# Compressed scores of two heads in one product of 64 columns, and the first operand parts of causal attention made in front of one meeting instead of two

## What is computed

```python
s = jnp.einsum('bqghd,bngd->bghqn', qb, k_cmp) * scale
p_cmp = _masked_softmax(s - slopes * dist, dist >= 0)
o_cmp = jnp.einsum('bghqn,bngd->bqghd', p_cmp.astype(v_cmp.dtype), v_cmp)
...
s = jnp.einsum('bqghd,bgqmd->bghqm', qb, k_sel) * scale
p = _masked_softmax(s - slopes * dist, dist >= 0)
o_slc = jnp.einsum('bghqm,bgqmd->bqghd', p.astype(v_sel.dtype), v_sel)
...
s = jnp.einsum('bqghd,bkgd->bghqk', qb, kw) * scale
p = _masked_softmax(s - slopes * wd.astype(jnp.float32), wmask)
o_win = jnp.einsum('bghqk,bkgd->bqghd', p.astype(vw.dtype), vw)
o = gb[..., 0:1] * o_cmp + gb[..., 1:2] * o_slc + gb[..., 2:3] * o_win
```

## Time and profile before

| | us |
|---|---|
| median of 3 runs | 3345.44 |
| lowest and highest of them | 3343.83, 3346.9 |
| the profiled execution | 3342.76 |
| its span in the trace | 3341.0 |
| PE busy in the span | 3247.5 (97%) |
| DVE, ACT, POOL busy | 1785.4 (53%), 1297.1 (39%), 205.7 (6%) |

### The profile page before, as it was taken

One profiled execution on the slowest core, in us unless ns is written; L12 is line 12 of the kernel. 1 busy time (PEld: TensorE's weight loads), 2 busy tenths in 40 slices (PEclk: granted clock), 3 DMA queues, 4 the chain that ended last, 5 costly groups with the idle time before them and its releaser, 6 DMA issues.

```text
span 3341.0 us, 41312 instructions
## 1 busy us (share of the span) xinstructions
PE 3247.5 (97%) x15343; PEld 2620.3 (78%) x15343; DVE 1785.4 (53%) x2671; ACT 1297.1 (39%) x1849; POOL 205.7 (6%) x230
## 2 busy tenths in 40 slices
PE   8989998999999999999999999999999999999998
PEld 6668976888888888876688888888888668888887
DVE  7357696445553455335765555345553566555532
ACT  4227755233332333323266333333322325633332
POOL 1001100000000000010110000010000011010000
PEclk9959999999999999999999999999999999999999
DMA  5320033333333333332312333333333322233332
GB/s 127 87 67 1 2 82 87 94 94 94 98 96 93 95 94 99 93 106 70 76 30 69 99 91 97 92 98 93 97 93 96 84 58 53 64 95 94 94 93 65
DMA packets 518489, 276.53 MB, mean 83 GB/s; under 512 B 39499, under 2 KB 510383, under 8 KB 518226
## 3 DMA queue, kind: packets, MB, share of 16 engines
q1 hardware_dynamic: 513154, 262.77, 28.6%
q0 software_dynamic: 3840, 11.26, 1.4%
q10 hardware_dynamic: 1360, 0.66, 0.1%
HBM read 264.11 MB, written 2.14 MB: 80 GB/s over the span
## 4 chain that ended last, share of the span: by engine, by line
PE 89%; DVE 7%; ACT 2%; issue 1%; DVEq 0%; DMA 0%; POOL 0%; ACTq 0%; POOLq 0%
PE bank L375 25%; PE bank L377 24%; PE bank L376 24%; PE bank L968 5%; PE bank L949 4%; PE bank L957 3%; PE bank L2386 1%; DVE wlo L351 1%; PE bank L1685 1%; PE bank L2359 1%; PE bank L2371 0%; DVE xc L1891 0%; DVE std L2571 0%; PE bank L687 0%; PE bank L1704 0%
## 5 line engine op out<-in xcount | busy, mean ns | idle before, releaser
L375 PE MATMUL bank<-hhi,whi 128*128 128x512 f32 (+1 forms) x2504 | 991.9, 396 | 7.5 <-DVE wlo L351 5.1
L377 PE MATMUL bank<-hlo,whi 128*128 128x512 f32 (+1 forms) x2504 | 977.0, 390 | 0.0
L376 PE MATMUL bank<-hhi,wlo 128*128 128x512 f32 (+1 forms) x2504 | 976.7, 390 | 0.0
L351 DVE TENSOR_TENSOR wlo<-raw,whi 128x1024 fp32r<-128x1024 f32 x485 | 608.9, 1258 | 585.0 <-ACT whi L344 576.2
L344 ACT CAST whi<-raw 128x1024 fp32r<-128x1024 f32 x485 | 505.1, 1046 | 408.6 <-PE bank L377 395.0
L375 PEld LDWEIGHTS bank<-hhi,whi 128*128 128x128 f32 (+1 forms) x2504 | 470.6, 188 | 147.3 <-issue 43.5
L376 PEld LDWEIGHTS bank<-hhi,wlo 128*128 128x128 f32 (+1 forms) x2504 | 470.7, 188 | 99.6 <-issue 3.4
L377 PEld LDWEIGHTS bank<-hlo,whi 128*128 128x128 f32 (+1 forms) x2504 | 470.1, 188 | 100.3
L375 PE MATMUL bank<-uhi,whi 128*128 128x512 f32 x880 | 348.6, 396 | 0.0
L376 PE MATMUL bank<-uhi,wlo 128*128 128x512 f32 x880 | 348.0, 395 | 0.0
L377 PE MATMUL bank<-ulo,whi 128*128 128x512 f32 x880 | 348.0, 395 | 0.0
(11 more groups left out here) (444 smaller groups left out, 3623.7 us busy)
## 6 DMA issues: line engine op xcount, KB each, us to landing
raw<-in_ffn_w_gate SPq DMA_DIRECT2D x88, 512.0 KB, 4.0
raw<-in_ffn_w_up SPq DMA_DIRECT2D x88, 512.0 KB, 3.8
raw<-in_w_in SPq DMA_DIRECT2D x78, 512.0 KB, 3.8
raw<-in_ffn_w_down SPq DMA_DIRECT2D x64, 512.0 KB, 4.1
raw<-in_w_out SPq DMA_DIRECT2D x24, 512.0 KB, 4.2
raw<-in_ffn_w_down SPq DMA_DIRECT2D x32, 384.0 KB, 3.5
raw<-in_w_gate SPq DMA_DIRECT2D x22, 512.0 KB, 4.1
raw<-in_w_up SPq DMA_DIRECT2D x22, 512.0 KB, 3.8
```

The costliest lines, as they stand in the source:

```text
L351: k.nc.vector.tensor_tensor(k.wlo[:, slot, :], k.raw[:, slot, :], k.whi[:, slot, :].bitcast(F32), ALU.subtract)\
L375: mm(out, whi, hi(kc), start=start and i == 0, stop=False)
L376: mm(out, wlo, hi(kc), start=False, stop=False)
L377: last = mm(out, whi, lo(kc), start=False, stop=stop and i == kcs - 1)
```

## The change

In `compressed_attention`, one product streams the 64 columns of the two groups that share a chunk of `q`, so that a tile takes 8 products in place of 16. The zeros in `kcmp` keep the two heads apart. The output goes to two blocks of 32 columns that lie 128 columns apart in the bank.

`stacked` and `keys` are allocated beside `q`. A new function `first_parts` has DVE make the parts of group 0 (both branches) and of heads 0 and 1 at the end of the stage of compressed attention, behind its last instruction there. The `handover` inside `causal_attention` is gone, and so are the entries of `head_at`, `keys_at` and `ready` for these parts. The making of the other parts is moved into two helpers and keeps its steps.

```diff
--- before.py
+++ after.py
@@ -1324,6 +1324,7 @@
                         handover(k)
 
                 q, dist = sb("q", [P, KC, T], F32, q_mem), sb("dist", [P, T], F32, q_mem)
+                stacked, keys = sb("qparts", [P, 2, T], F32R, q_mem), sb("kparts", [P, 2, 2, 2, T], F32R, q_mem)
                 cmp_mem = ExitStack()
                 bias, mask = sb("cmpbias", [P, TB, NH * 32], F32, cmp_mem), sb("cmpmask", [P, TB, 32], F32, cmp_mem)
 
@@ -1337,9 +1338,10 @@
                 handover(k)
             with cmp_mem as mem:
                 compressed_attention(k, mem, q, kcmp, vcmp, gates, otok, bias, mask)
+                first_parts(k, q, kT, stacked, keys)
                 handover(k)
             with ExitStack() as mem:
-                causal_attention(k, mem, q, dist, kT, vals, gates, otok)
+                causal_attention(k, mem, q, dist, kT, vals, gates, otok, stacked, keys)
                 outputs = k.pt_copied.all(), k.o_read.all(), k.o_added.all()
                 handover(k, pe_waits=False)
             q_mem.close()
@@ -1426,14 +1428,42 @@
     normalize(k, items, back, scales[1], NORM1_HEADS)
 
 
-def causal_attention(k, mem, q, dist, kT, vals, gates, otok):
+def head_parts(k, dve, q, stacked, h):
+    rows, c = query_rows(h)
+    k.nc.vector.tensor_copy(stacked[rows, h % 2, :], q[rows, c, :]).then_inc(*k.q_high.up())
+    dve.wait_ge(*k.q_high.all())
+    k.nc.vector.tensor_tensor(stacked[HD - rows.start:P - rows.start, h % 2, :], q[rows, c, :],
+                              stacked[rows, h % 2, :].bitcast(F32), ALU.subtract).then_inc(*k.q_parts.up())
+
+
+def key_parts(k, dve, kT, keys, g, b):
+    rows, _ = query_rows(HPG * g)
+    halves = (rows, slice(HD - rows.start, P - rows.start))
+    src, hi, lo = kT[rows, 2 * b + g // 2, :], keys[:, g % 2, b, 0, :], keys[:, g % 2, b, 1, :]
+    for to in halves:
+        last = k.nc.vector.tensor_copy(hi[to], src)
+    last.then_inc(*k.k_high.up())
+    dve.wait_ge(*k.k_high.all())
+    for to in halves:
+        last = k.nc.vector.tensor_tensor(lo[to], src, hi[rows].bitcast(F32), ALU.subtract)
+    last.then_inc(*k.k_parts.up())
+
+
+def first_parts(k, q, kT, stacked, keys):
+
+    @k.block.vector
+    def _(dve):
+        for b in range(2):
+            key_parts(k, dve, kT, keys, 0, b)
+            head_parts(k, dve, q, stacked, b)
+
+
+def causal_attention(k, mem, q, dist, kT, vals, gates, otok, stacked, keys):
 
 
     nc = k.nc
     sb = lambda name, shape, dt=F32: mem.enter_context(nc.sbuf_tensor(k.name(name), shape, dt))
     bias = sb("bias", [P, 2, T])
-    stacked, keys = sb("qparts", [P, 2, T], F32R), sb("kparts", [P, 2, 2, 2, T], F32R)
-    handover(k)
     groups, builds = [], []
     for h in range(NH):
         g = h // HPG
@@ -1447,40 +1477,24 @@
                             values=[vals[b][:, i, g, :] for i in range(t + 1)]) for t in range(TB)],
                 out=otok[:, :, h * HD:(h + 1) * HD], add=True, factor=gates[:, :, 3 * h + 1 + b]))
 
-    other = lambda rows: slice(HD - rows.start, P - rows.start)
-    head_at = {8 * h: h + 1 for h in range(NH - 1)}
-    head_at[-1] = 0
+    head_at = {8 * h: h + 1 for h in range(1, NH - 1)}
     keys_at = {32 * g + 3 + 8 * b: (g + 1, b) for g in range(NG - 1) for b in range(2)}
-    keys_at.update({-1: (0, 0), 0: (0, 1)})
     order = [keys_at[t] for t in sorted(keys_at)]
-    ready = {8 * h: [k.q_parts.at(h + 1)] for h in range(NH)}
-    for g in range(NG):
+    ready = {8 * h: [k.q_parts.at(h - 1)] for h in range(2, NH)}
+    for g in range(1, NG):
         for b in range(2):
             ready.setdefault(32 * g + 4 * b, []).append(k.k_parts.at(order.index((g, b)) + 1))
 
     def both_parts(dve, t):
         if t in keys_at:
             g, b = keys_at[t]
-            rows, _ = query_rows(HPG * g)
-            src, hi, lo = kT[rows, 2 * b + g // 2, :], keys[:, g % 2, b, 0, :], keys[:, g % 2, b, 1, :]
             if g >= 2:
                 dve.wait_ge(*k.qk_done.at(32 * (g - 1)))
-            for to in (rows, other(rows)):
-                last = nc.vector.tensor_copy(hi[to], src)
-            last.then_inc(*k.k_high.up())
-            dve.wait_ge(*k.k_high.at(order.index((g, b)) + 1))
-            for to in (rows, other(rows)):
-                last = nc.vector.tensor_tensor(lo[to], src, hi[rows].bitcast(F32), ALU.subtract)
-            last.then_inc(*k.k_parts.up())
+            key_parts(k, dve, kT, keys, g, b)
         if t in head_at:
             h = head_at[t]
-            rows, c = query_rows(h)
-            if h >= 2:
-                dve.wait_ge(*k.qk_done.at(8 * (h - 1)))
-            nc.vector.tensor_copy(stacked[rows, h % 2, :], q[rows, c, :]).then_inc(*k.q_high.up())
-            dve.wait_ge(*k.q_high.at(h + 1))
-            nc.vector.tensor_tensor(stacked[other(rows), h % 2, :], q[rows, c, :], stacked[rows, h % 2, :].bitcast(F32),
-                                    ALU.subtract).then_inc(*k.q_parts.up())
+            dve.wait_ge(*k.qk_done.at(8 * (h - 1)))
+            head_parts(k, dve, q, stacked, h)
 
     attention(k, groups, mem, builds, ready=ready, splits=both_parts)
 
@@ -1669,6 +1683,7 @@
 
 def compressed_attention(k, mem, q, kcmp, vcmp, gates, otok, bias, mask):
 
+
     nc = k.nc
     sb = lambda name, shape: mem.enter_context(nc.sbuf_tensor(k.name(name), shape, F32))
     s, pT = sb("cs", [P, 2, NH * 32]), sb("cpT", [P, 2, NH * 32])
@@ -1681,9 +1696,11 @@
         def scores(t):
             if t >= 2:
                 pe.wait_ge(*k.cs_biased.at(t - 1))
-            for h in range(NH):
-                last = nc.tensor.matmul(k.bank[t % 2][:, 32 * h:32 * h + 32], q[:, query_rows(h)[1], t * P:(t + 1) * P],
-                                        kcmp[:, h // HPG, :], start=True, stop=True)
+            out = k.bank[t % 2][:, :].rearrange("p (g h n) -> p g h n", g=NG, h=HPG)
+            for c in range(KC):
+                g = 2 * (c // HPG)
+                last = nc.tensor.matmul(out[:, g:g + 2, c % HPG, :], q[:, c, t * P:(t + 1) * P], kcmp[:, g:g + 2, :],
+                                        start=True, stop=True)
             last.then_inc(*k.cs_done.up())
         scores(0)
         scores(1)
```

## The result

The changed kernel's median is 3328.69 us (five runs, 3319.18 to 3329.75), that of the kernel before 3343.83 in the runs beside it (3342.11 to 3346.9). The ratio is 0.994, with a 95% interval from 0.9925 to 0.9955. The kernel is faster by some 20 us by the ratio and by 15 us by the medians; 15.0 were forecast. The interval of the ratio spans some 15 to 25 us. Taken by the ratio, 3345.44 x 0.994 is 3325.4, a tenth of a microsecond under the low end of my range. The profiled execution is the fastest of the five, 3319.18, with a span of 3317.4 and a mean granted clock of 0.984 (0.978 before).

What follows compares the result with a forecast made beforehand. PE, with 89% of the chain of waits, was taken as the bound. Gains 8.4 + 0.2 + 3.8 + 1.3 = 13.7 us gave 3329.1 from the profiled execution or 3331.7 from the median; forecast 3330.4 us, range 3325.5 to 3336.5.

Steps and rivals of the forecast that it cites:

- A product of 64 columns: Compressed-stage scores: a record of 64 columns takes 0.215 us, so half the records take half the time; split output costs nothing.
- My second rival: Compressed-stage scores: a 64-column record with split output costs twice a 32-column one, leaving 3340.3 us; 7 in 100.
- Tiles 0 to 2: Start of the compressed stage: fewer score records, then PE waits for DVE and transposes near 217.5; gain 8.4 us.
- The first rival: Compressed-stage scores: the clock rises during them, a record costs 0.114 us, total gain 18.3 us to 3324.5; 8 in 100.
- Tile 3 and the rest of the stage: Compressed stage: tile 3's 16 records at low clock gain 0.2 us; the rest unchanged, 1 us either way for the clock.
- First parts and one meeting: Between the stages: parts hidden before one meeting bring the causal stage's first score product forward by 3.8 us.
- The cover: End of the compressed stage: last value products and ACT's copies hide DVE's parts, which end 1.15 us before ACT's last copy.
- The pause behind step 0: Start of the causal stage: DVE no longer stops for 3.44 us between steps 0 and 1; gain 1.3 us.
- my upper bound: Causal stage, DVE's pause behind step 0: at most the whole pause is gained, 3.4 us.
- Theory 2: Between the stages, set out for the follow-up runs: closing the idle gap keeps TensorE's clock high, worth 3 to 4 us every run.
- My own bound for "most": Whole kernel: largest gain 18.4 us, from the profiled execution 3324.4 us.
- my fourth rival: Start of causal attention: TensorE stays at 1.2 GHz, from 41 us more on slower by over 0.2%, some 3353; 2 in 100.

Runs made afterwards that it cites:

- one_pair_filled: one_pair plus matmuls with unread results in PE's waits around the first parts, against the changed kernel; median 3328.82 us, ratio 0.996 to the kernel before.
- one_pair: Changed kernel with only the first pair of parts before the meeting, the second pair behind step 0 again; median 3329.59 us, ratio 0.9958 to the kernel before.
- after_again: The changed kernel itself, unaltered, measured and profiled once more; median 3324.33 us, ratio 0.9957 to the kernel before.
- two_meetings: Changed kernel with a second meeting put back behind the first; median 3328.0 us, ratio 0.9947 to the kernel before.

## Why the prediction was right or wrong

**A product of 64 columns: right.** 0.22 us a record, twice the columns for nothing, and the split output costs nothing either. My second rival (7 in 100) fell with it.

**Tiles 0 to 2: right.** Forecast 8.4 us. From the first product to the first transposes it took 20.50 us before and 12.08 after, 8.4 less. DVE is what is late next, as worked out. The first rival (the clock rises in the scores) didn't come: granted clock 0.50 for all 48 records.

**Tile 3 and the rest of the stage: mis-sized.** I took 0.2 us and left the clock behind it at 1 either way. It was 3.4: 1.3 for the scores of tile 3 (2.36 for 3.65), 0.5 for the transposes behind them (0.46 for 0.92), 1.7 for the value products of tile 3 (2.01 for 3.67). All beyond the 0.2 comes from the clock, which stood higher under these products than I had taken: tile 3's scores at 0.72, the two groups behind at 1.00. The last group before, then the wait and the two groups that answer to it after:

```profile
248.18 3.66 PE L1704 MATMUL bank<-vcmp,cpT 128*128 128x256 f32 x8 [0.80 <-ACT cpT L1721]
```

```profile
226.61 1.99 PE L1721 MATMUL bank<-vcmp,cpT 128*128 128x256 f32 x8 [0.67 <-ACT cpT L1738]
231.00 1.00 PE L1714 MATMUL bank<-ident,cs 128*128 128x128 f32 x4 [2.39 <-DVE cs L1776]
...
238.10 1.99 PE L1721 MATMUL bank<-vcmp,cpT 128*128 128x256 f32 x8 [0.80 <-ACT cpT L1738]
```

The value products of tile 1 (226.61) also took 1.8 us less than before, and that gave nothing, since PE then waited 2.39 us for DVE. The step that failed is "I leave the 18 us to the end of the stage as they are, with 1 us either way for the clock", together with the low clock for tile 3. I had priced the clock for one group of products and not for the bursts behind it. With the 1.8 us for tile 3 and that 1 us my sum allowed 2.8 at most, and a burst of value products at the high clock alone is worth 1.8.

**First parts and one meeting: right.** 3.8 forecast, 3.79 measured. The cover held, though thinner than I had it.

**The pause behind step 0: mis-sized, and for a wrong reason.** The second step that failed is "the rest of DVE's pause lay beside PE's queue". I took 1.3 us from PE's idle time between 257 and 262. The runs show 3.8 for pause and clock together. one_pair_filled puts the pause at 3.5 us by itself, the length of DVE's six operations, my upper bound. At the low clock PE looked busy beside the pause, since each product took twice as long, but that queue wasn't the bound, DVE was. Here PE's idle time undercounted the wait, because PE ran slowly enough to fill part of it. The low clock has a price of its own mainly without the pause: 1.0 and 1.3 us for 3.7 and 4.8 us of it (149.3 and 149.6 for 148.3). With the pause 6.8 us of it cost 0.3 (one_pair for one_pair_filled). The two hide each other, and so neither theory had it. Theory 2 is right that the clock stays high at this place where gap and pause are both gone (in all seven profiles with one meeting, no pause and a step of at most 1.2 us to line 949, three of them with idle products), and wrong on the price.

**The sum.** 13.7 forecast for these stages, 19.4 in the profile. 3.2 of the difference are the clock within the compressed stage, 2.5 the pause (with the clock). The 4.2 us that the execution shows beyond lie behind these stages, and the second profile doesn't have them. The median lies 9.5 us above the profiled execution. Where the other four runs spent that I can't say, as they have no trace, but the three traces under after_again lie 12.8 us apart in the part behind the edit. So it is luck that the medians of the first measurement lie 15.1 us apart, where I had forecast 15.0: two of my terms were 5.7 us short together. In the second set the medians lie 19.8 apart (3344.12 and 3324.33), near the 19.4 of the stages.

**The range.** My own bound for "most" was 3324.4, and I wrote 3325.5 as the low end. The 3325.4 by the ratio lies between the two. The stages' 19.4 us are also more than the 18.4 of that bound, so the terms were too narrow and not only the range.

**Slower than before.** The low clock at the start of the causal stage lasted 4.8 us at most where all parts stood in front, and cost 1.3; the 27 us from which my fourth rival would eat the gain were never near. Its rule that x us at the low clock cost x / 2 was too dear here: 3.7, 4.8 and (with the pause) 6.8 us cost 1.0, 1.3 and 0.3, as one would expect where DVE and not PE sets the pace.

## What to carry to other kernels

Where the spacing of products of few columns doesn't depend on their columns, as with 32 and 64 here, joining two of them halves the time; the next bound is then the engine that reads the results, and its chain gives the gain. Before a pause of an engine within a pipeline is priced at the idle time that it leaves on another, look which of the two sets the pace there: DVE was busy nearly without a break at the start of this stage, and its pause of 3.4 us cost 3.5, not 1.3. Work hidden under another engine's last operations stays hidden only as long as those stay slow: a faster clock left 2.3 us of it uncovered in two_meetings. And one fast execution is no measure of an edit: 4.2 of the 23.6 us between the two profiles weren't the edit's, which a second profile of the same kernel showed.

## What the runs showed of the hardware

The places where the granted clock falls repeat. In after_again the low stretches of the two stages begin at 179.8 and 231.0 us and last 44.4 and 6.8, as in the first profile of the changed kernel (180.0 and 231.2). Which value products are slow goes with small shifts of the start: at a start of the scores at 205.4 to 205.7 the last ones ran at 2.4 GHz in four profiles and the stage took 35.7; at 205.8 they ran at 1.2 GHz in three, and it took 37.4; at 207.2 and 207.6 the last two groups ran fast, and it took 35.3. These are the profiles without idle products ahead of the last value products and with 64 columns; that the start decides it is a reading of nine profiles, not an experiment.

Products of 64 columns that kept PE busy for 10.3 us left the clock at 1.2 GHz, like the 20.7 us of 32 columns before. Bursts of 256 columns of 3.7 us were followed by a high clock in some places (tile 0, before) and not in others (tile 1, before). The Trainium skill, "TensorE: Matmul & The Clock Gate", Part 1, ties the release to sustained activity. These traces disagree as far as a matmul queue without a gap wasn't followed by a release in either case.
